# Row sums of the first attention's exponentials taken over by VectorE, and its constant matmuls left out

## The reference

```python
ATTN_PATTERNS = ((128, 1), (512, 4), (2048, 16))      # window, dilation
HEAD_GROUPS = (6, 5, 5)                                # 16 heads of 64
...
s = jnp.einsum('bnqrhd,bnkrhd->bnrhqk', qb, kc)
s = jnp.where(mask, s, NEG_INF)
m = jnp.max(s, axis=-1, keepdims=True)
e = jnp.exp(s - m)
den = jnp.sum(e, axis=-1, keepdims=True)
p = e / den
o = jnp.einsum('bnrhqk,bnkrhd->bnqrhd', p, vc)
lse = m + jnp.log(den)
...
alpha = softmax over the three groups of logsumexp(lse over the group's heads) - log(n_heads)
merged = o of each group * 3 * alpha of the group
```

## Time and profile before

| | us |
|---|---|
| median of 3 runs | 3017.51 |
| lowest, highest | 3017.27, 3019.92 |
| the profiled execution | 3022.45 |
| its span in the trace | 3020.7 |
| PE busy of the span | 2978.3 (99%) |
| DVE busy | 2178.2 (72%) |
| ACT busy | 1275.6 (42%) |
| the 22 steps, first exponential to last `probsT_lo` | 634.07 to 685.88 |
| TensorE's mean granted clock over the span | 0.995 |

### The profile page before, as it was taken

One profiled execution on the slowest core, in us unless ns is written; L12 is line 12 of the kernel. 1 busy time (PEld: TensorE's weight loads), 2 busy tenths in 40 slices (PEclk: granted clock), 3 DMA queues, 4 the chain that ended last, 5 costly groups with the idle time before them and its releaser, 6 DMA issues.

```text
span 3020.7 us, 46546 instructions
## 1 busy us (share of the span) xinstructions
PE 2978.3 (99%) x17415; PEld 2601.4 (86%) x17415; DVE 2178.2 (72%) x3215; ACT 1275.6 (42%) x1903; POOL 128.6 (4%) x121
## 2 busy tenths in 40 slices
PE   8999999999999999999999999999999999999998
PEld 7888888887888889998877899988998878799987
DVE  7577765765777678785688787867775478788753
ACT  4333223465332245452345554425454244654442
POOL 0000000000000000000031000000000013000000
PEclk9999999999999999999999999999999999999999
DMA  4355553213555533343322133442333322123332
GB/s 162 99 191 194 188 196 99 84 43 95 176 181 192 191 106 103 104 148 114 92 81 63 57 105 103 155 153 84 106 108 103 101 79 84 36 91 104 105 105 76
DMA packets 263452, 351.94 MB, mean 117 GB/s; under 512 B 16770, under 2 KB 208500, under 8 KB 263312
## 3 DMA queue, kind: packets, MB, share of 16 engines
q1 hardware_dynamic: 241344, 270.57, 28.8%
q0 software_dynamic: 21488, 79.09, 8.0%
q10 hardware_dynamic: 480, 0.35, 0.0%
HBM read 348.76 MB, written 2.10 MB: 116 GB/s over the span
## 4 chain that ended last, share of the span: by engine, by line
PE 87%; DVE 9%; ACT 2%; issue 2%; DMA 0%; POOL 0%; DVEq 0%; SPq 0%; ACTq 0%
PE bank L2237 18%; PE bank L2239 18%; PE bank L2238 18%; PE bank L2378 9%; PE bank L2380 9%; PE bank L2381 9%; DVE w_lo L1324 1%; PE bank L2298 1%; PE bank L2260 1%; PE bank L2263 1%; PE bank L2261 1%; DVE a_score L1824 1%; ACT w_hi L754 0%; DVE h_f L1379 0%; DVE h_lo L1385 0%
## 5 line engine op out<-in xcount | busy, mean ns | idle before, releaser
L1324 DVE TENSOR_TENSOR w_lo<-raw,w_hi 128x1024 fp32r<-128x1024 f32 x322 | 393.8, 1224 | 510.8 <-ACT w_hi L754 508.0
L754 ACT ACTIVATE w_hi<-raw 128x1024 fp32r<-128x1024 f32 x348 | 368.6, 1059 | 894.9 <-PE bank L2239 844.8
L2237 PE MATMUL bank<-h_hi,w_hi 128*128 128x512 f32 x1376 | 541.8, 394 | 4.3 <-POOL w_lo L702 2.6
L2239 PE MATMUL bank<-h_hi,w_lo 128*128 128x512 f32 x1376 | 537.1, 390 | 0.0
L2238 PE MATMUL bank<-h_lo,w_hi 128*128 128x512 f32 x1376 | 536.5, 390 | 0.0
L2237 PE MATMUL bank<-act_hi,w_hi 128*128 (+1 forms) x1120 | 437.8, 391 | 0.0
L2239 PE MATMUL bank<-act_hi,w_lo 128*128 (+1 forms) x1120 | 436.1, 389 | 0.0
L2238 PE MATMUL bank<-act_lo,w_hi 128*128 (+1 forms) x1120 | 435.8, 389 | 0.0
L2237 PEld LDWEIGHTS bank<-h_hi,w_hi 128*128 128x128 f32 x1376 | 259.0, 188 | 61.5 <-issue 8.1
L2239 PEld LDWEIGHTS bank<-h_hi,w_lo 128*128 128x128 f32 x1376 | 258.8, 188 | 54.8
L2238 PEld LDWEIGHTS bank<-h_lo,w_hi 128*128 128x128 f32 x1376 | 259.2, 188 | 52.5
(11 more groups left out here) (382 smaller groups left out, 5695.3 us busy)
## 6 DMA issues: line engine op xcount, KB each, us to landing
raw<-in_ffn_w_in_dram SPq DMA_DIRECT2D x176, 512.0 KB, 3.5
ada_w<-in_ada_w_dram POOLq DMA_DIRECT2D x72, 1024.0 KB, 5.6
raw<-in_ffn_w_out_dram SPq DMA_DIRECT2D x88, 512.0 KB, 3.6
raw<-in_ffn_w_gate_dram SPq DMA_DIRECT2D x44, 512.0 KB, 3.8
raw<-in_ffn_w_up_dram SPq DMA_DIRECT2D x44, 512.0 KB, 3.9
raw<-in_ffn_w_down_dram SPq DMA_DIRECT2D x44, 512.0 KB, 4.3
raw<-in_mix_w_in_dram SPq DMA_DIRECT2D x44, 512.0 KB, 3.6
raw<-in_attn_w_qkv_dram SPq DMA_DIRECT2D x24, 512.0 KB, 3.7
```

Source lines behind the costliest of these rows:

```text
L754: nc.scalar.activation(w_hi[:, nb % SPL, :], raw_slab(nb), ACT.Copy).then_inc(s_hi, 1)
L1324: V.tensor_tensor(w_lo[:, nb % SPL, :], raw_slab(nb), w_hi[:, nb % SPL, :].bitcast(F32), ALU.subtract).then_inc(s_lo, 1)
L2237: T.matmul(dst, wh, mh, start=first, stop=False)
L2239: return T.matmul(dst, wl, mh, start=False, stop=last)
```

## The change

The row sums of steps 0 to 19 are no longer made by ScalarE's accumulators. VectorE makes them with `tensor_reduce` over `P`, in iteration s between `mask_step(s + 3)` and `probs_lo(s)`: one instruction over all 512 columns for lower and dilated steps, two (128 and 256 columns) for upper steps. The last two steps keep the accumulators. A new semaphore, `s_rowsum`, says that a step's sums are there; ScalarE waits on it before it overwrites `P` two steps later, and so do the readers of `sums`. (`SUMS_BY_ACT` is the number of steps whose sums are NOT made by ScalarE, 20.) The line with `keep_warm` inside the steps is gone; the 22 constant matmuls behind the steps (line 2817) stay.

```diff
--- before.py
+++ after.py
@@ -335,6 +335,7 @@
         s_scmm = sem("scores_mm")
         s_masked = sem("scores_masked")
         s_exp = sem("exp_done")
+        s_rowsum = sem("row_sums_of_a_step_ready")
         s_tr = sem("probs_transposed")
         s_pth = sem("probsT_hi_ready")
         s_pt = sem("probsT_ready")
@@ -500,6 +501,21 @@
 
             at = 24 * n + u if u < 4 * DILATED else 48 + 40 * n + u - 4 * DILATED
             return a1["sums"][:, at:at + 1]
+
+        SUMS_BY_ACT = len(A0) - 2
+
+        def row_sums(step):
+
+            blocks = step[2]
+            if blocks[0][4] == blocks[1][4]:
+                groups = [blocks]
+            else:
+                groups = [[block] for block in blocks]
+            for group in groups:
+                u, _, _, off, n, _ = group[0]
+                c = len(group)
+                at = 24 + u if u < 4 * DILATED else 48 + 40 + u - 4 * DILATED
+                yield (a1["sums"][:, at:at + c], off, n, c)
 
         def width(step):
             return sum(n for _, _, _, _, n, _ in step[2])
@@ -1195,9 +1211,15 @@
                     act.wait_ge(s_masked, s + 1)
                     if s >= 2:
                         act.wait_ge(s_tr, s - 1)
+                        if s - 2 < SUMS_BY_ACT:
+                            act.wait_ge(s_rowsum, s - 1)
                     for u, _, _, off, n, _ in A0[s][2]:
-                        ins = nc.scalar.activation(b_["P"][:, s % 2, off:off + n], bank[STEP_BANKS[s % 4]][:, off:off + n], ACT.Exp,
-                                                   scale=-1.0, bias=sum_col(0, u), accum_out=sum_col(1, u))
+                        if s < SUMS_BY_ACT:
+                            ins = nc.scalar.activation(b_["P"][:, s % 2, off:off + n], bank[STEP_BANKS[s % 4]][:, off:off + n], ACT.Exp,
+                                                       scale=-1.0, bias=sum_col(0, u))
+                        else:
+                            ins = nc.scalar.activation(b_["P"][:, s % 2, off:off + n], bank[STEP_BANKS[s % 4]][:, off:off + n], ACT.Exp,
+                                                       scale=-1.0, bias=sum_col(0, u), accum_out=sum_col(1, u))
                     ins.then_inc(s_exp, 1)
                     if s:
                         probs_hi(s - 1)
@@ -2058,6 +2080,12 @@
                         split_lo(N0["out0"] + 1)
                     if s + 3 < n_steps:
                         mask_step(s + 3)
+                    if s < SUMS_BY_ACT:
+                        dve.wait_ge(s_exp, s + 1)
+                        for dst, off, n, c in row_sums(A0[s]):
+                            ins = V.tensor_reduce(dst, a1["P"][:, s % 2, off:off + c * n].rearrange("p (c n) -> p c n", n=n),
+                                                  AX_X, ALU.add)
+                        ins.then_inc(s_rowsum, 1)
                     probs_lo(s)
                     if s - 1 in DONE_AT and DONE_AT[s - 1] in O_VECTOR:
                         o_out(DONE_AT[s - 1])
@@ -2074,6 +2102,7 @@
                     return bank[1][:, 0:20 * NB].rearrange("p (b h) -> p b h", h=20)[:, :, 10 * n:10 * n + 10]
 
                 dve.wait_ge(s_exp, n_steps)
+                dve.wait_ge(s_rowsum, SUMS_BY_ACT)
                 V.tensor_copy(nmx[:, :, here], own(0))
                 link(V.tensor_scalar(den[:, :, here], own(1), third, None, ALU.mult))
                 V.reciprocal(coef[:, :, here], den[:, :, here])
@@ -2796,12 +2825,12 @@
                 for s in range(n_steps):
                     if s >= 2:
                         pe.wait_ge(s_pt, s - 1)
-                    keep_warm({0: 6, 2: 6, 3: 4, 6: 6, 7: 6, 9: 6, 11: 6}.get(s, 0), 2 + s % 2)
                     pe.wait_ge(s_exp, s + 1)
                     for k in range(width(A0[s]) // P):
                         ins = T.transpose(bank[2 + s % 2][:, k * P:(k + 1) * P], bufs["P"][:, s % 2, k * P:(k + 1) * P], ident)
                     ins.then_inc(s_tr, 1)
                     if s == n_steps - 1:
+                        pe.wait_ge(s_rowsum, SUMS_BY_ACT)
                         for r in range(4):
                             ins = T.transpose(bank[7][0:20, r::4], bufs["sums"][:, 48 + r::4], ident)
                         ins.then_inc(s_sumT, 1)
```

## The result

The changed kernel takes 3025.78 us (median of 10 runs, 3024.51 to 3027.19) against 3018.07 for the kernel before (10 runs, 3014.79 to 3020.17): a ratio of 1.0025 with a 95% interval of 1.0017 to 1.0033, slower by 7.7 us.

What follows compares the result with a forecast made beforehand. The prediction took a loop between TensorE and VectorE, 4.61 us per dilated pair, as the bound. Row sums +6.2, constants -2.4 and clock +4.5 gave +8.3 on 3017.51, so 3025.8 us, range 3018.8 to 3031.

Steps and rivals of the forecast that it cites:

- What bounds the steps: First attention's 22 steps: a TensorE-VectorE loop holds a dilated pair at 4.61 us, ScalarE's own cycle being 4.53.
- The row sums, +6.2: VectorE's reduces in odd iterations lie wholly in the loop, 5.6 us; with 0.6 for the end, +6.2.
- The added wait on ScalarE: Exponentials of step s + 2 wait for sums of step s; costs nothing extra except +0.6 at the end.
- The accumulators, 0: Dropping 56 reads saves ScalarE 0.05 to 0.09 us a block, but ScalarE is not in the loop: 0.
- The constants, -2.4: Forty matmuls gone from the steps; 2.4 us come back at steps 3, 7 and 11, ends 0 and 4.0.
- The sum at an unchanged clock, +3.8: Row-sum side +6.2 less 2.4 for the constants, with the clock as it is: +3.8 us.
- The clock, +4.5: TensorE's clock falls in three more places, steps 0 to 3, 5 to 7 and dilated pairs, 1.5 us each.
- Why it falls: Without constants, and with every loop 0.6 longer in which TensorE stands still, stretches like that before 657.0 come up.
- the clock stays as before: Rival: loop longer, but VectorE's longer steps leave TensorE enough to do; 3021.3, from 3019 to 3023; chance 0.27.
- the reduces are hidden: Rival: reduces fill part of VectorE's 14.2 us of waits and the constants' 2.4 come back; 3015.1 to 3017.5; chance 0.06.
- ScalarE is the limiter: Rival: ScalarE, not the loop, limits; each dropped read is worth its full duration, 14.6 us go, 3002.9; chance 0.04.
- stay low through the stage: Rival: the clock stays low, TensorE's 2.9 us part of the loop doubles, eleven loops give +32, 3053; chance 0.05.

Runs made afterwards that it cites:

- e4: Kernel before with the accumulators of steps 0 to 19 dropped, nothing in their place, sums set to 1.0, constants kept: 3017.45 us, ratio 0.9999.
- e6: e1 with VectorE making the row sums of even steps 0 to 18 only, odd steps keeping the accumulators: 3021.30 us, ratio 1.0010.
- e1: Changed kernel with the 40 constant matmuls put back, row sums staying on VectorE: 3028.61 us, ratio 1.0036.
- e5: e1 with three buffers of P instead of two: 3023.88 us, ratio 1.0021.
- e3: e1 with each step's reduce placed behind `probsT_lo` instead of in front of it: 3033.88 us, ratio 1.0055.
- e7: e3 with three buffers of P instead of two: 3019.90 us, ratio 1.0002.
- e2: Kernel before without the 40 constant matmuls, accumulators kept: 3018.11 us, ratio 1.0001.
- e8: e7 without the constant matmuls: 3021.71 us, ratio 1.0010.

## Why the prediction came out right, point by point

The time forecast was 3025.8 and the range 3018.8 to 3031; measured were 3025.8. That it agrees to the digit is luck: the terms under it were off on both sides, and the base was too, since the forecast was +8.3 on 3017.51 and the measurement +7.7 on 3018.07.

- **What bounds the steps.** Right for the pair that was read, 15 to 17. The loop of TensorE and VectorE held it at 4.61; the reduce in an odd iteration made it 5.20, where 5.2 was forecast. e4 shows that ScalarE, with its 4.53, did not hold it (4.61 without any accumulator), e6 that a reduce in even iterations leaves it at 4.6. It was too simple to take all dilated pairs for this one: 11 to 13 and 13 to 15 were in part ScalarE's before (e4), and in the changed kernel 13 to 15 is VectorE's alone, with the even step's reduce on the chain.
- **The row sums, +6.2.** Measured by e1: +5.4 +-0.9. The price of a reduce was right (0.60, and 0.52 for an upper step's two: they start at 636.37 and `probsT_lo` at 636.89). In 634:692 VectorE is busy for 47.4 us, where about 47 was forecast, and ScalarE for 39.1, under the 40.
- **The added wait on ScalarE.** Here a step failed. "It stretches nothing that the loop does not already stretch, except at the end" is contradicted by the chain after, which goes from reduces over exponentials to transposes in iterations 3, 7 and 11. What this costs in the changed kernel no run measured: a third buffer was not tried with the reduce in front and the constants out. With the constants kept it is 1.2 +-1.0 us (e5 against e1), of which the end, predicted at 0.6, is 0.62 (pair 17 to 19, 4.97 and 4.35); in e1's trace the chain passes through this wait at the end alone. With the reduce behind `probsT_lo` the same wait was worth 9.1 +-1.2 us (e3 against e7). I had taken a wait to be harmless by looking only at where it would be seen, and not at the cycle that it closes.
- **The accumulators, 0.** Nearly right: e4 gives -0.8 +-0.7 for all of them, and 0.08 us a block of ScalarE's time was within the 0.05 to 0.09.
- **The constants, -2.4.** Measured -1.4 +-0.7 from before (e2), 3.6 - 5.4 = -1.8 +-1.0 with the sums on VectorE, and 0.0 - 0.8 = -0.8 +-0.9 with three buffers (e8 against e7). The size was too large, by some 0.6 to 1.6.
- **The sum at an unchanged clock, +3.8.** Measured +3.6 +-0.8, from two terms that were both too large.
- **The clock, +4.5.** Measured +3.5: 12.5 us more at the low clock, for 0.28 each. I had three pieces of 3.4 us (10.2) at 1.5, that is 0.44 for each microsecond. The amount was a little low, the price too high: a piece costs 0.95 by the fit, 0.84 and 1.34 by the pairs of traces. I took the price from three groups of instructions on the chain (one of them, called 24 score matmuls, is 14 in its row), as if every microsecond that they grew had come through. Which part of the low time is off the chain was not measured. The places were forecast near 640 and 650; the falls came at 638 and 659.
- **Why it falls.** I gave two reasons, the missing constants and the longer loops. Low clock by kernel, constants kept against left out: accumulators 17.1 and 20.9, reduce in front 32.8 and 29.6, reduce behind with three buffers 17.6 and 27.4. The reduce in front raises it with the constants and without them. The missing constants raise it in two kernels of three, and in e2's trace the steps hold 3.4 us of it, as before. Executions of one kernel scatter in it by 3 to 12 us, so single differences are weak. The split of the 3.5 us between the two reasons is not settled.

Of the rivals, "the clock stays as before" would have been 3021.3 and is out by the traces of the steps; "the reduces are hidden" is what e7 reaches (+0.8), by two edits that the change did not make; "ScalarE is the limiter", with its 12.2 us for the reads, is refuted by e4; and the clock did not stay low through the stage (13.7 of 58.5 us).

## What to carry to other kernels

Moving work from a busy engine to one with idle time pays only if the idle time lies where the work is put: write down the cycle of waits that sets the period, then ask of each insertion whether it is inside. Do so for each stretch, since the next pair of steps may hang on another engine. Test the whole idea first by leaving the work out altogether (e4: 0.8 us was all there was to win). A new reader of a double buffer adds a cycle, from the writer over everything in front of the reader and back, and a third buffer may be worth more than the place of the instruction. And an edit that makes TensorE wait in small pieces can be paid a second time in its clock: in the changed kernel nearly as much as the first time, in e7 not by its mean (17.6 us low against 17.1).

## What the runs showed of the hardware

- An accumulator read on ScalarE lasts 0.22 us but takes 0.08 to 0.09 of the engine, since it overlaps the exponential in front of it; 56 fewer of them were worth 0.8 us +-0.7 here.
- A reduce of 128x512 on VectorE lasts 0.67 to 0.68 us, and the next instruction starts 0.60 after it, the same as for `probsT_lo` of that size.
- The time at the low clock costs 0.28 us (+-0.02) for each microsecond, over 159 executions of eleven kernels that do mostly the same. Single executions of one kernel differ by 5 us and more through this alone, so differences of 2 or 3 us between kernels show only when the granted clock of each run is taken out.
- Spells at the low clock in the steps lasted from 3.4 to 10.2 us, and the same kernel had them in other number and length from one execution to the next (changed kernel: 13.7 and 10.2 us in all).
